# Three modulation pieces moved from the first FFN to the end of the retention stage, and four instructions reordered around the first layer

## The chip, the cores and the metric

One core of a Trainium2 chip (trn2) runs the whole program in one launch. The metric is device time in microseconds (us), lower is better. Engines are written as the profile writes them: PE (TensorE matmul), PEld (its weight load), DVE (VectorE), ACT (ScalarE), POOL (GpSimd), SP (SyncE, which issues the weight DMAs).

## The reference

A two-layer mixer block is followed by a two-layer conditioned block. All of it is float32, 256 tokens, model width 1024. What matters here, cut:

```python
# first block, layer 0
h = rmsnorm(x, mix_norm_even)
cq, ckv, k_rope, rq, rk, rv, rg = split(h @ w_in_even)      # 1024 x 2720
a = mla(cq, ckv, k_rope, positions, ...)                    # 8 heads, softmax attention
r = silu(rg) * rmsnorm(retention_fwd + retention_bwd)       # 8 heads of 64
x = x + concatenate([a, r]) @ w_out_even                    # 1024 x 1024
x = x + conv_ffn(x, ...)                                    # 1024 -> 2 x 2816 -> 1024
# first block, layer 1: gated linear attention, then a conv_ffn
# second block: every layer is modulated by a condition that no token depends on
mod_x = split(silu(c)     @ w_mod[layer] + b_mod[layer], 6) # 1024 x 6144, two layers
mod_c = split(silu(c_ctx) @ w_mod[layer] + b_mod[layer], 6)
```

## The kernel before, in words

**Weights.** Weight matrices come from DRAM in pieces of up to 1 MB (128 x 2048 float32) through a ring of six slots. SP loads piece n as soon as the user of piece n-6 has released it, strictly in the order in which PE uses the pieces. Most products are made in three passes: ACT casts the piece to a rounded copy (`weights_hi`, L1439, `ring_hi`, three buffers), DVE subtracts it from the piece (`weights_lo`, L2066, `ring_r`), and PE multiplies high by high, high by low and low by high (`mm3`, L408). `hi_upto(n)` and `lo_upto(n)` issue those casts on ACT and DVE up to the n-th split piece; where the call stands in an engine's program is where the cast runs, since each engine takes its instructions in order. The normed input is split in the same way: DVE writes `h`, ACT rounds it (`h_hi`), POOL subtracts (L1329, `h_lo`).

**Modulation pieces.** The product with `w_mod` depends on no token. It is cut into 48 pieces of 1 MB, and `fill(n)` spreads them over the first block. On PE a fill is eight small matmuls (printed as 16 in the profile, 128x256, into bank 7 of PSUM), and then `turn_mod` of the piece before it (4 printed, 128x2). On ACT a fill is a wait for those matmuls, a copy `res<-ps` 128x256 that frees bank 7, and the copy `mods<-ps` 128x4 of the piece before it. So the next fill's matmuls can't start before ACT has made the copy. How many pieces go where is in `FILL` and `FFN_FILL`: 16 in attention, one per step, 4 in retention, 9 in the first FFN (1 ahead of it, 8 in its up steps).

**Opening.** PE makes the input projection in column blocks (`tokens`), each in two halves of 512 rows, one split piece per half. DVE casts piece 0, norms the input (L2046), casts piece 1 with `lo_upto(j + 2)`, then computes the rotary angles from the positions (L2025 to L2244, signal `setup_dve`), two small scalings (L2246, L2248), and the casts of pieces 2 and 3. ACT waits for `setup_dve` (L1606) and then makes sine, cosine and some decay terms, and only behind these the copies of block 0 and the cast of piece 4.

**Attention** has 16 steps (`attend_mla`). At each, PE issues the scores of step n+2, a fill, the transposes of step n's probabilities, and the product of step n-1. The scores of step n+2 use the bank of step n, so they wait for ACT's exponential of step n (L1486). ACT's order in a step is: exponential; in odd steps an exponential of a retention decay (L1491), which waits for DVE (L2115); in steps 6, 8, 10 and 12 a copy of transposed retention inputs (L1439, `h<-ps` 128x512); then the fill's two copies.

**Retention** goes over four head pairs p. PE: `ret_scores`, `ret_pv`, `ret_back` (transposes, L837, and one fill for each p). ACT: copy `ret_oT`, square (L1691), square root (L1477), fill. DVE: decay multiply (L2344), reduction (L2355), gate multiply (L2358), scale (L2364, signal `heads_mix`). Then `turn_mix` transposes the mixed features in four groups (L490), ACT and DVE split them (`pairs_hi`, L1439 and L1565; `pairs_lo`, L2192), and `out_project` multiplies with `w_out_even`. `keep_warm(u, n)` issues n bf16 matmuls whose result is not used (L448).

**First FFN** (`ffn0`): 22 up steps, each one 1 MB piece and 48 matmuls, DVE's convolution (L2409 to L2411), then 11 down pieces.

Of the kernel before, what the change touches and what calls it, by code (L numbers as in the profile page):

```python
# [89 lines left out]
def expert_pieces(x):  # L90
# [6 lines left out]
HALVES = [16, 8]  # L97
MOD_PIECES = 48

FILL = {"attention": 16, "ret": 4, "ffn0": 9, "odd": 1, "gla_gates": 2, "gla": 8,  # L100
        "odd_mix": 3, "ffn1": 5}
FFN_FILL = [(2, 4, 7, 9, 12, 14, 17, 20), range(4, 18, 4)]
PARTS = {"even_act": 0, "even_dve": 0, "odd_act": 7, "odd_dve": 5}
assert sum(FILL.values()) == MOD_PIECES
ONE = [(0, q) for q in range(4)]
# [75 lines left out]
def build(nc, A, out):  # L181
    ctx = ExitStack()
    with ctx:
# [5 lines left out]
        def sig(name):  # L189
            if name not in sems:  # L190
                sems[name] = ctx.enter_context(nc.semaphore(name))
            return sems[name]
# [28 lines left out]
        def col(name, i):  # L221
            return cols[:, COLS[name] + i:COLS[name] + i + 1]
# [3 lines left out]
        warm = sb("warm", [P, 1])  # L226
# [19 lines left out]
        mix0 = area(areaB, 4096, TT, D)  # L246
# [82 lines left out]
        first_split = {}  # L329
# [28 lines left out]
        def _(pe):  # L358
# [86 lines left out]
            def keep_warm(u, n):  # L445

                for _ in range(n):
                    pe.matmul(ps[:, u.bank, :], warm_l, warm_r, start=True, stop=True, skip_group_check=True)  # L448
# [30 lines left out]
                            release(m)  # L479
                    release_with(us[-1])  # L480

            def turn_mix(tag, src, fp, n, bank=None, warm=2):

                u = take(tag, "mixT", fp, bank=bank)
                keep_warm(u, warm)
                pe.wait_ge(sig("heads_mix"), n)
                for f in (2 * fp, 2 * fp + 1):
                    for t in range(TT):
                        at = (f % 2) * T + t * P
                        m = pe.transpose(ps[:, u.bank, at:at + P], src[:, t, f * P:(f + 1) * P], ident)  # L490
                full(m, u)
# [276 lines left out]
            for g in range(3):  # L768
                u = take("mla_cT", g)
# [8 lines left out]
            for half in range(2):  # L778
                v = chunk(Piece("mla_w_uq", 0, 0, CQ, half * 384, (half + 1) * 384), 3 * 384, "p (k c) -> p k c", k=3)
                for t in range(TT):  # L780
                    u = take("mla_q", t, half)
# [6 lines left out]
            for half in range(2):  # L788
                for t in range(TT):
                    u = take("mla_kv", t, half)  # L790
# [6 lines left out]
            for i, (name, src) in enumerate((("qT", qh), ("kT", kx))):  # L797
                pe.wait_ge(sig("mla_heads"), i + 1)
                for t in range(TT):
                    for g in range(2):  # L800
                        u = take("mla", name, t, g)
# [52 lines left out]
            ret_pv(3)  # L854
            turn_mix("even", mix0, 2, 4, 2)
            ret_back(3)
            turn_mix("even", mix0, 3, 6, 3, 8)
            out_project("even_out", ("w_out_even", 0), 1, 2 * (MIXED["even"] + TT), "ffn0", True)


# [70 lines left out]
            for d in range(2):  # L931
                for t in range(TT):
                    u = take("gla_la", d, t)
                    full(mm(ps[:, u.bank, :], gaT[0:2 * GR + 1, t * P:(t + 1) * P], wg[0:2 * GR + 1, d, :]), u)
            parts(1, 1, "odd")
            for t in range(TT):
                u = take("gla_kT", t)
# [7 lines left out]
            for d in range(2):  # L945
                pe.wait_ge(sig("gla_la"), d + 1)
                for t in range(TT):
                    u = take("gla_kd", d, t)
# [7 lines left out]
            for n in range(2 * GH):  # L956
# [13 lines left out]
                u = take("gla_A", n)  # L970
# [20 lines left out]
            for l in range(2):  # L991
# [9 lines left out]
                u = take("gates", l)  # L1001
# [4 lines left out]
                for c in range(2):  # L1006
                    v = split_chunk(Piece(*w, 0, D, 768 + c * 256, 768 + (c + 1) * 256), "p (k c) -> p k c", k=8)
                    for m2 in range(2):
                        u = take("conv", l, 2 * c + m2)
# [12 lines left out]
                for t in both:  # L1022
                    if t < 2 or l == 0:
                        u = take("aqT", l, t)
                        for j in range(4):
                            src = ro[:, t, j * P:(j + 1) * P] if t < 2 else p2[:, t, j * P:(j + 1) * P]
# [86 lines left out]
            u = take("rank")  # L1113
# [321 lines left out]
        def _(act):  # L1435
# [43 lines left out]
            def attend_mla():  # L1479
                for n, (t, hd) in enumerate(MLA):  # L1480
                    L.wait("att_m", n + 1)
                    if n >= 3:

                        look(act, "mla", "pT", n - 3)
                    u = look(act, "mla", "s", n)
                    free(L, act.activation(mla_p[:, n % 3, :], ps[:, u.bank, 0:T], ACT.Exp, bias=stat[:, n:n + 1],  # L1486
                                           scale=MQK ** -0.5, accum_out=stat[:, 16 + n:17 + n]), u, "att_p")
                    if n % 2:
                        x = n // 2
                        L.wait("ret_e", x + 1)  # L1490
                        L.tell(act.activation(decay[:, x, :, :], decay[:, x, :, :], ACT.Exp), "ret_d")  # L1491
                    if n - 1 in RET_AT:
                        t, g = divmod(RET_AT.index(n - 1), 2)
                        u = look(act, "ret_T", t, g)
                        free(L, copy(rT[:, 4 * g:4 * g + 4, t * P:(t + 1) * P],
                                     ps[:, u.bank, :].rearrange("p (a b) -> p a b", a=4)), u, "ret_T")
                    fill(1)

            def attend_pairs(l):

# [42 lines left out]
            def hi_upto(n):  # L1543

                while his[0] < n:
                    weights_hi(his[0])
                    his[0] += 1
# [8 lines left out]
            def pairs_hi(tag, fps, gain):  # L1556

                for fp in fps:
                    u = look(act, tag, "mixT", fp)
                    if gain(2 * fp) is None:  # L1560
                        L.tell(copy(h_hi[:, 0, 2 * fp:2 * fp + 2, :],
                                    ps[:, u.bank, :].rearrange("p (a b) -> p a b", a=2)), "mixT_hi")
                        continue
                    for f in (2 * fp, 2 * fp + 1):
                        L.tell(act.activation(h_hi[:, 0, f, :], ps[:, u.bank, (f % 2) * T:(f % 2 + 1) * T], ACT.Copy,  # L1565
                                              scale=gain(f)), "mixT_hi")
# [19 lines left out]
            def fill(n):  # L1586

                for i in range(filled[0], filled[0] + n):
                    u = look(act, "mod", i)
                    free(L, copy(modrow[:, i % 2, :], ps[:, u.bank, 0:256]), u, "mod_row")  # L1590
                    if i:
                        turned_mod(i - 1)
                filled[0] += n
# [93 lines left out]
            for p in range(4):  # L1687
                u = look(act, "ret_b", p)
                if p >= 2:
                    L.wait("heads_sumsq", 1 + p)  # L1690
                L.tell(act.activation(rsq[:, p % 2, :, :], ps[:, u.bank, 0:T].rearrange("p (a b) -> p a b", a=4),  # L1691
                                      ACT.Square), "heads_sq")
                if p == 2:
                    hi_upto(first_split["even_out"] + 1)
                if p < 3:
                    ret_oT(p + 1)
                L.wait("heads_sumsq", 3 + p)
                rstd(stat[:, 4 * p:4 * p + 4], RD)
                act.sem_inc(sig("heads_rstd"), 1)
                if p < FILL["ret"]:  # L1700
                    fill(1)
                if p == 1:
                    pairs_hi("even", (0, 1), lambda f: None)
            pairs_hi("even", (2, 3), lambda f: col("ret_g", f - 4))
            def project_out(tag, mix, tiles, gain, norm, n, after=None):
                j = first_split[tag]
# [313 lines left out]
        def _(dve):  # L2020
# [50 lines left out]
            def lo_upto(n):  # L2071

                while los[0] < n:
                    weights_lo(los[0])
                    los[0] += 1
# [148 lines left out]
            j = first_split["even_in"]  # L2224
            lo_upto(j + 1)
            norm(1, lambda hf, k: col("mix_even", k), split=True)
            lo_upto(j + 2)

            L.wait("pos_loaded", 16)
            S(copy(posf, posi[:, :]))  # L2230
# [106 lines left out]
            for n in range(6):  # L2337
                if n < 4:
                    for hd in range(2):
                        u = look(dve, "ret_s", n, hd)  # L2340
                        L.wait("ret_d", 2 * n + hd + 1)
                        if n >= 2:
                            look(dve, "ret_o", n - 2)
                        free(L, STT(out=sdec[:, n % 2, hd, :], in0=ps[:, u.bank, :], scalar=RD ** -0.5,  # L2344
                                    in1=decay[:, 2 * n + hd, :, :].rearrange("p a b -> p (a b)"), op0=ALU.mult,
                                    op1=ALU.mult), u, "ret_sdec")
                if n == 3:
                    pairs_lo("even", (0, 1), lambda f: None)
                if 1 <= n <= 4:
                    p = n - 1  # L2350
                    if n == 4:
                        lo_upto(first_split["even_out"] + 1)
                    u = look(dve, "ret_b", p)
                    L.wait("heads_sq", 3 + p)
                    S(dve.tensor_reduce(stat[:, 4 * p:4 * p + 4], rsq[:, p % 2, :, :], AX.X, ALU.add))  # L2355
                    dve.sem_inc(sig("heads_sumsq"), 1)
                    a = EVEN["rg"] + P * p
                    free(L, TTN(mix0[:, :, 512 + P * p:640 + P * p], ps[:, u.bank, 0:T].rearrange("p (a b) -> p a b", a=2),  # L2358
                                pe_[:, :, a:a + P], ALU.mult), u)
                if n >= 2:  # L2360
                    p = n - 2
                    inverted("heads_rstd", 4 + p, stat[:, 4 * p:4 * p + 4])
                    v = mix0[:, :, 512 + P * p:640 + P * p].rearrange("p t (h c) -> p t h c", h=2)
                    L.tell(TTN(v, v, bc(stat[:, 4 * p:4 * p + 4].rearrange("p (t h) -> p t h", t=TT), 3, [P, TT, 2, RD]),  # L2364
                               ALU.mult), "heads_mix")
# [552 lines left out]
```

## Time and profile before

| | |
|---|---|
| median of 3 runs | 2642.38 us (2640.11 to 2644.3) |
| the profiled execution | 2644.3 us, span 2642.5 us |
| PE busy | 2476.5 us, 94% |
| DVE / ACT / POOL busy | 1666.2 / 1280.4 / 533.0 us |
| mean granted TensorE clock | 0.963 |

The span is from the first to the last instruction of the profiled execution; 1.8 us of its time lie around it. PE's share of the span is high, so what matters is the idle time on PE and the matmuls that it issues, stage by stage. The opening lies at 0 to 57 us, attention at 113 to 167, retention to 194, the output projection to 220, the norm to 234, the first FFN's up steps to 370.

### The profile page before, as it was taken

The numbers are of one execution on the slowest core, as the hardware profiler recorded it, in microseconds if no ns is written. First come the engines' busy times: TensorE is split into PE (matmuls) and PEld (weight loads), VectorE is DVE, ScalarE is ACT, GpSimd is POOL, SyncE is SP. The second block draws the span as 40 slices with busy tenths as digits, with TensorE's granted clock in tenths as the row PEclk, the third lists the DMA queues.
The fourth block names the chain that finished last, engine by engine and source line by source line (L and its number), as shares of the span: only waits on it lengthen the run. The fifth ranks groups of instructions, "written<-read, shape, count | busy, mean of one in ns | idle before, by whom it ended". The sixth has DMA issues, their size and how long they took to land.

```text
span 2642.5 us, 37437 instructions
## 1 busy us (share of the span) xinstructions
PE 2476.5 (94%) x14360; PEld 2060.7 (78%) x14360; DVE 1666.2 (63%) x1755; ACT 1280.4 (48%) x1541; POOL 533.0 (20%) x406
## 2 busy tenths in 40 slices
PE   7999999999999998779999989889999999999997
PEld 5668998768998865558889968567887887887886
DVE  6555764446775566643222256657888888888886
ACT  6453444544343445432222133545677676677674
POOL 1003541002541000022002630001232232222321
PEclk9999999999999998689999989888999999999998
DMA  5575654554663310012222213015899889899894
GB/s 197 204 253 185 232 205 154 177 193 150 216 209 106 112 64 9 3 62 96 96 96 96 88 49 127 25 66 193 336 337 353 336 342 348 334 348 352 322 363 174
DMA packets 71328, 502.75 MB, mean 190 GB/s; under 512 B 8176, under 2 KB 8688, under 8 KB 11248
## 3 DMA queue, kind: packets, MB, share of 16 engines
q1 hardware_dynamic: 70128, 496.75, 51.3%
q0 software_dynamic: 1024, 3.61, 0.4%
q8 instruction: 116, 1.90, 0.3%
q14 instruction: 60, 0.49, 0.1%
HBM read 499.28 MB, written 1.05 MB: 189 GB/s over the span
## 4 chain that ended last, share of the span: by engine, by line
PE 83%; DVE 9%; ACT 5%; issue 2%; POOL 1%; DMA 1%; DVEq 0%; ACTq 0%; SPq 0%; PEldq 0%
PE ps L408 80%; DVE ring_r L2066 1%; DVE h L2044 1%; POOL h_r L1329 1%; DVE h L2042 1%; DVE areaA L2036 1%; PE ps L1153 1%; PE ps L448 1%; ACT ring_hi L1439 1%; DVE h L2046 1%; ACT h L1517 1%; DVE areaB L2546 0%; ACT extra_r L1577 0%; DVE temp L2129 0%; DVE h L2632 0%
## 5 line engine op out<-in xcount | busy, mean ns | idle before, releaser
L1439 ACT ACTIVATE ring_hi<-ring 128x2048 fp32r<-128x2048 f32 x427 | 807.3, 1893 | 511.4 <-PE ps L408 504.8
L2796 DVE TENSOR_TENSOR ring_r<-ring,ring_hi 128x2048 fp32r<-128x2048 f32 x264 | 625.2, 2373 | 119.0 <-ACT ring_hi L1439 117.1
L408 PE MATMUL ps<-ring_hi,extra_r 128*128 128x512 f32 (+2 forms) x1808 | 611.4, 395 | 31.8 <-DVE ring_r L2066 19.0
L2066 DVE TENSOR_TENSOR ring_r<-ring,ring_hi 128x2048 fp32r<-128x2048 f32 (+3 forms) x163 | 388.2, 2382 | 220.6 <-ACT ring_hi L1439 206.5
L408 PE MATMUL ps<-extra_r,ring_hi 128*128 128x256 f32 (+1 forms) x1432 | 465.8, 325 | 33.6 <-POOL h_r L1329 20.5
L408 PE MATMUL ps<-h_r,ring_hi 128*128 128x256 f32 (+1 forms) x1432 | 459.6, 321 | 0.0
L408 PE MATMUL ps<-extra_r,ring_r 128*128 128x256 f32 (+1 forms) x1432 | 459.3, 321 | 0.0
L408 PEld LDWEIGHTS ps<-ring_hi,extra_r 128*128 128x128 f32 x1808 | 343.6, 190 | 109.3 <-DVE ring_r L2066 22.0
L408 PE MATMUL ps<-ring_r,extra_r 128*128 128x512 f32 (+2 forms) x1104 | 426.4, 386 | 0.0
L408 PEld LDWEIGHTS ps<-extra_r,ring_hi 128*128 128x128 f32 x1432 | 275.4, 192 | 58.5 <-POOL h_r L1329 23.6
L408 PEld LDWEIGHTS ps<-h_r,ring_hi 128*128 128x128 f32 x1432 | 275.7, 193 | 19.1
L408 PEld LDWEIGHTS ps<-extra_r,ring_r 128*128 128x128 f32 x1432 | 275.2, 192 | 19.0
L1385 POOL TENSOR_TENSOR areaA_r<-areaA,cst 128x256 fp32r<-128x256 f32 x88 | 123.0, 1397 | 588.2 <-ACT areaA L1962 588.2
L408 PEld LDWEIGHTS ps<-ring_r,extra_r 128*128 128x128 f32 x1104 | 211.4, 191 | 38.7 <-issue 0.2
L1329 POOL TENSOR_TENSOR h_r<-h,extra_r 128x256 fp32r<-128x256 f32 x80 | 85.4, 1083 | 449.2 <-ACT extra_r L1439 449.2
L408 PE MATMUL ps<-ring_hi,h_r 128*128 128x512 f32 (+2 forms) x400 | 151.2, 378 | 0.0
L408 PE MATMUL ps<-ring_hi,areaA_r 128*128 128x512 f32 x352 | 137.6, 391 | 6.0 <-ACT areaA L1962 6.0
L408 PE MATMUL ps<-ring_hi,areaB_r 128*128 128x512 f32 x352 | 139.8, 397 | 0.0
L408 PE MATMUL ps<-ring_r,areaA_r 128*128 128x512 f32 x352 | 138.0, 392 | 0.0
L408 PE MATMUL ps<-areaA_r,ring_hi 128*128 128x256 f32 x704 | 127.0, 283 | 0.0
L408 PE MATMUL ps<-areaB_r,ring_hi 128*128 128x256 f32 x704 | 124.4, 280 | 0.0
L2704 DVE TENSOR_TENSOR areaA<-ps,areaB 128x512 f32<-128x512 f32 x22 | 15.2, 692 | 166.9 <-PE ps L408 166.9
(350 smaller groups left out, 3339.4 us busy)
## 6 DMA issues: line engine op xcount, KB each, us to landing
ring<-in_experts SPq DMA_DIRECT2D x264, 1024.0 KB, 4.9
ring<-in_stream SPq DMA_DIRECT2D x202, 1024.0 KB, 4.9
ring<-in_stream SPq DMA_DIRECT2D x6, 512.0 KB, 3.6
areaB<-in_consts POOLq DMA_DIRECT2D x3, 512.0 KB, 4.0
ring<-in_stream SPq DMA_DIRECT2D x2, 576.0 KB, 3.7
res<-in_xT SPq DMA_DIRECT2D x1, 1024.0 KB, 5.7
res<-in_ctxT POOLq DMA_DIRECT2D x1, 1024.0 KB, 7.8
out_xT<-h SPq DMA_DIRECT2D x4, 256.0 KB, 2.2
```

The source lines that it names most:

```text
L408: return pe.matmul(o, l, r, start=start, stop=stop, skip_group_check=True)
L448: pe.matmul(ps[:, u.bank, :], warm_l, warm_r, start=True, stop=True, skip_group_check=True)
L1153: m = pe.transpose(ps[:, 3, s * P:(s + 1) * P], mprod[:, n % 2, s * P:(s + 1) * P], ident)
L1329: pool.tensor_tensor(h_lo[:, hf, k, :], h[:, hf, k, :], h_hi[:, hf, k, :].bitcast(F32), ALU.subtract).then_inc(sig("h_lo"), 1)
L1385: pool.tensor_tensor(hi, mturn[:, n % 2, :], ones[:, 0:1].broadcast_to([P, NM]), ALU.mult).then_inc(sig("moe_hi"), 1)
L1439: return act.activation(dst, src, ACT.Copy)
L1517: free(L, act.activation(pair_p[:, 2 * (n % 2) + hd, 0:w.keys * P], ps[:, u.bank, 0:w.keys * P], ACT.Exp, bias=pair_neg[:, i:i + 1], scale ...
L2036: S(dve.reciprocal(rs, rs))
L2042: S(TTN(h[:, hf, k:k + 4, :], res[:, hf, k:k + 4, :], bc(rs[:, hf * T:(hf + 1) * T], 1, [P, 4, T]), ALU.mult))
L2044: ins = TS(h[:, hf, k, :], h[:, hf, k, :], gain(hf, k), shift(hf, k), ALU.mult, ALU.add)
L2066: L.tell(TTN(ring_lo[:, s, 0:n], ring[:, s, 0:n], ring_hi[:, j % HIS, 0:n].bitcast(F32), ALU.subtract), "weights_lo")
L2796: TTN(ring_lo[:, s, :], ring[:, s, :], ring_hi[:, j % HIS, :].bitcast(F32), ALU.subtract).then_inc(sig("weights_lo"), 1)
```

## The change

Three of the first FFN's nine modulation pieces are made at the end of retention, behind `ret_back(3)` on PE and ahead of the last two feature groups on ACT; the eight warm-up matmuls there become two. The FFN's remaining in-step fills stand at every fourth step. On ACT, each attention step's fill comes before the decay exponential and the transposed-input copy. The two casts of the output projection's first piece move back on both engines: on ACT from ahead of `ret_oT(3)` to behind the fill of p = 2, on DVE from ahead of the last reduction to behind it. In the opening, DVE's cast of piece 1 is no longer made right behind the norm but by the later `lo_upto(j + 4)`.

```diff
-FILL = {"attention": 16, "ret": 4, "ffn0": 9, "odd": 1, "gla_gates": 2, "gla": 8,
+FILL = {"attention": 16, "ret": 4, "even_mix": 3, "ffn0": 6, "odd": 1, "gla_gates": 2, "gla": 8,
         "odd_mix": 3, "ffn1": 5}
-FFN_FILL = [(2, 4, 7, 9, 12, 14, 17, 20), range(4, 18, 4)]
+FFN_FILL = [range(4, 22, 4), range(4, 18, 4)]
...
-            def turn_mix(tag, src, fp, n, bank=None, warm=2):
+            def turn_mix(tag, src, fp, n, bank=None):
                 u = take(tag, "mixT", fp, bank=bank)
-                keep_warm(u, warm)
+                keep_warm(u, 2)
...
             turn_mix("even", mix0, 2, 4, 2)
             ret_back(3)
-            turn_mix("even", mix0, 3, 6, 3, 8)
+            fill(FILL["even_mix"])
+            turn_mix("even", mix0, 3, 6, 3)
             out_project("even_out", ("w_out_even", 0), 1, 2 * (MIXED["even"] + TT), "ffn0", True)
...
# ACT, attend_mla
                     free(L, act.activation(mla_p[:, n % 3, :], ps[:, u.bank, 0:T], ACT.Exp, bias=stat[:, n:n + 1],
                                            scale=MQK ** -0.5, accum_out=stat[:, 16 + n:17 + n]), u, "att_p")
+                    fill(1)
                     if n % 2:
...
                         free(L, copy(rT[:, 4 * g:4 * g + 4, t * P:(t + 1) * P],
                                      ps[:, u.bank, :].rearrange("p (a b) -> p a b", a=4)), u, "ret_T")
-                    fill(1)
...
# ACT, retention
-                if p == 2:
-                    hi_upto(first_split["even_out"] + 1)
                 if p < 3:
                     ret_oT(p + 1)
...
                 if p < FILL["ret"]:
                     fill(1)
+                if p == 2:
+                    hi_upto(first_split["even_out"] + 1)
                 if p == 1:
                     pairs_hi("even", (0, 1), lambda f: None)
+            fill(FILL["even_mix"])
             pairs_hi("even", (2, 3), lambda f: col("ret_g", f - 4))
...
# DVE, opening
             norm(1, lambda hf, k: col("mix_even", k), split=True)
-            lo_upto(j + 2)
 
             L.wait("pos_loaded", 16)
...
# DVE, retention
-                    if n == 4:
-                        lo_upto(first_split["even_out"] + 1)
                     u = look(dve, "ret_b", p)
                     L.wait("heads_sq", 3 + p)
                     S(dve.tensor_reduce(stat[:, 4 * p:4 * p + 4], rsq[:, p % 2, :, :], AX.X, ALU.add))
                     dve.sem_inc(sig("heads_sumsq"), 1)
+                    if n == 4:
+                        lo_upto(first_split["even_out"] + 1)
```

## Rows read from the trace of the kernel before

**Rows 1.** The page: the span.
```profile
span 2642.5 us, 37437 instructions
```

**Rows 2.** Timeline of PE in the opening: start us, us, engine, line, operation, idle before.
```profile
27.80 0.50 PE L408 MATMUL ps<-ring_hi,extra_r 128*128 128x512 f32 x1 [1.09 <-DVE ring_r L2066]
...
44.28 0.80 PE L408 MATMUL ps<-ring_hi,extra_r 128*128 128x512 f32 x1 [5.42 <-DVE ring_r L2066]
```

**Rows 3.** Windows: length, busy of PE, PEld, DVE, ACT, POOL; PEclk, DMA share, GB/s.
```profile
44.20:47.50 3.30, 3.22 (x8) 2.55 (x9) 2.65 (x3) 0.49 (x2) 0.00 (x0) 0.50 0.01 2
```

**Rows 4.** Timeline of DVE in the opening.
```profile
25.14 2.60 DVE L2066 TENSOR_TENSOR ring_r<-ring,ring_hi 128x2048 fp32r<-128x2048 f32 x1
27.79 0.58 DVE L2025 CAST temp<-positions 128x2 f32<-128x2 int32 x1
...
31.04 0.17 DVE L2248 TENSOR_SCALAR cols<-cols 128x8 f32<-128x8 f32 x1
...
41.94 4.62 DVE L2066 TENSOR_TENSOR ring_r<-ring,ring_hi 128x2048 fp32r<-128x2048 f32 x2 [0.16 <-DVE areaA L2025]
```

**Rows 5.** Timeline of POOL in the opening, window 26 to 27 us.
```profile
25.59 2.74 POOL L1329 TENSOR_TENSOR h_r<-h,extra_r 128x256 fp32r<-128x256 f32 x1
```

**Rows 6.** Timeline of ACT in the opening.
```profile
30.87 1.28 ACT L1606 ACT_TABLE_LOAD   x1 [3.30 <-DVE temp L2244]
```

**Rows 7.** Timeline of ACT in attention, steps 8 to 10.
```profile
141.42 0.60 ACT L1439 ACTIVATE h<-ps 128x512 f32<-128x512 f32 x1
143.13 0.38 ACT L1439 ACTIVATE res<-ps 128x256 f32<-128x256 f32 x1 [1.11 <-PE ps L408]
...
143.84 0.47 ACT L1486 ACTIVATE h<-ps,stat 128x256 f32<-128x256 f32 x1
...
145.86 0.63 ACT L1491 ACTIVATE extra<-extra 128x512 f32<-128x512 f32 x1 [1.45 <-DVE extra L2115]
...
147.02 0.17 ACT L1439 ACTIVATE mods<-ps 128x4 f32<-128x4 f32 x1
147.23 0.47 ACT L1486 ACTIVATE h<-ps,stat 128x256 f32<-128x256 f32 x1
```

**Rows 8.** Timeline of PE in attention: the fill of step 9.
```profile
145.09 1.07 PE L408 MATMUL ps<-ring,res 128*32 128x256 f32 x16
```

**Rows 9.** Timeline of ACT at the end of retention.
```profile
184.57 1.91 ACT L1439 ACTIVATE ring_hi<-ring 128x2048 fp32r<-128x2048 f32 x1
...
188.66 0.38 ACT L1691 ACTIVATE areaB<-ps 128x256 f32<-128x256 f32 x1
189.91 0.30 ACT L1477 ACTIVATE stat<-stat,cst 128x4 f32<-128x4 f32 x1 [0.88 <-DVEq L2356]
190.33 0.38 ACT L1439 ACTIVATE res<-ps 128x256 f32<-128x256 f32 x1
...
191.04 0.98 ACT L1565 ACTIVATE extra_r<-ps,cols 128x256 fp32r<-128x256 f32 x2
```

**Rows 10.** Timeline of DVE at the end of retention.
```profile
187.02 2.28 DVE L2066 TENSOR_TENSOR ring_r<-ring,ring_hi 128x2048 fp32r<-128x2048 f32 x1
189.34 0.42 DVE L2355 TENSOR_REDUCE stat<-areaB 128x4 f32<-128x256 f32 x1
```

**Rows 11.** Timeline of PE: the output projection's first matmul.
```profile
194.41 0.47 PE L408 MATMUL ps<-extra_r,ring_hi 128*128 128x256 f32 x1
```

**Rows 12.** Timeline of DVE in the first FFN: starts of three convolution steps.
```profile
250.00 0.54 DVE L2409 TENSOR_SCALAR areaB<-ps,cols 128x256 f32<-128x256 f32 x1 [2.46 <-PE ps L408]
...
255.75 0.54 DVE L2409 TENSOR_SCALAR areaB<-ps,cols 128x256 f32<-128x256 f32 x1 [0.82 <-PE ps L408]
...
263.15 0.54 DVE L2409 TENSOR_SCALAR areaB<-ps,cols 128x256 f32<-128x256 f32 x1 [2.46 <-PE ps L408]
```

**Rows 13.** Timeline of PE in layer 1: two fills.
```profile
521.54 1.49 PE L408 MATMUL ps<-ring,res 128*32 128x256 f32 x16 [2.43 <-ACT res L1439]
...
590.73 1.93 PE L408 MATMUL ps<-ring,res 128*32 128x256 f32 x16
```

## The prediction

> **What bounds the kernel now.** I read the page first for the span and the shares of the engines, then the list of PE's waits over 0 to 60, 110 to 170 and 230 to 380 us, then the timeline of each engine in the stages that the diff touches. PE is busy 94% of the span, so an edit matters only where it opens or closes an idle stretch of PE, or adds or removes matmuls. Four places are touched. In the opening PE stands still for 5.42 us until DVE has cast piece 4 [rows 2], and when it goes on its clock is at the lower of the two levels, 1.2 GHz, for the next 3.3 us [rows 3]. In attention every step runs round a ring of PE and ACT: exponential, scores, fill matmuls, the fill's two copies on ACT, the next exponential [rows 7, 8]. At the end of retention a chain on ACT and DVE leads to the first matmul of the output projection [rows 9 to 11]. In the first FFN's up steps PE has no idle time, and each fill makes a step longer.
>
> **The opening: earlier angles, a later cast of piece 1.** The position work on DVE runs from 27.79 to 31.21 us, 3.42 us, behind the cast of piece 1 that began at 25.14 [rows 4]. Without that cast it starts 2.65 us earlier. ACT's chain begins the moment it is told [rows 6], so it and the decay terms on DVE behind it come 2.65 us earlier too. The price: the cast of piece 1 now starts at 25.14 + 3.42 = 28.56. One such cast takes 2.31 us where POOL is quiet (half of 4.62 [rows 4]), so it ends at 30.9, and PE's second half starts at 30.95 instead of 27.80 [rows 2]. From 27.80 PE works without a break until 44.28 - 5.42 = 38.86, 11.06 us; the same work now ends at 42.0. The new gap ahead of it is about 4.2 us (3.15 more than the 1.09 that stands there). The clock fell in the gap of 5.42, so I let it fall here: half of 3.3 us at PEclk 0.50 is 1.65 us lost [rows 3]. PE then reaches piece 4 at 43.65. Piece 4's casts wait for PE to release a `ring_hi` buffer at the end of the slowed second half (30.95 + 5.6 + 1.65 = 38.2; 5.6 is my estimate of 24 of the matmuls of about 0.23 us), then take 1.92 on ACT and 2.31 on DVE: ready at 42.5, just in time. Before, PE reached the same point at 44.28 and then lost its own 1.65: 45.93. Gain 2.3 us. Bounds: nothing, if piece 4 is late all the same; 3.9 (45.93 - 42.0) if the clock holds in the new gap.
> While DVE's cast of piece 1 ran from 25.14 to 27.74, POOL's last subtraction took 2.74 us [rows 4, 5], and DVE's first position instruction, two elements wide, took 0.58 [rows 4]. The Trainium skill (SBUF — State Buffer, "Who interferes with whom") says that a DVE instruction with two SBUF inputs and a GpSimd one that reads SBUF take a shared port for the whole instruction, and the second fully blocks. By it the position work, now beside POOL's last subtraction, might start up to 0.9 us later and the gain be 1.4; by the rows alone it is 2.3, and I keep that.
>
> **Attention: the fill ahead of ACT's other work.** Before, the decay exponential sits in the time in which ACT waits for the fill's matmuls: they run until 145.09 + 1.07 = 146.16 [rows 8], and the exponential until 146.49 [rows 7]. It costs the ring only the 0.33 us by which it is late, because DVE delivers late. With the fill first, ACT's copy can start at 146.23, 0.07 behind the matmuls as in step 8 (0.38 long, the mods copy 0.5 after its start, ready for the next instruction 0.21 later: 147.02 to 147.23 [rows 7]), thus at 146.94. Then the decay exponential comes in the ring with its 0.63 and 0.03 of handover: next exponential at 147.60 instead of 147.23, +0.37. Seven odd steps have a next one: 2.6 us. In steps 6, 8, 10 and 12 the copy of 0.60 runs at 141.42, wholly inside the wait that ends at 143.13 [rows 7]. Moved behind the fill it lies bare between 143.81 and the exponential at 143.84: +0.63, four times, 2.5 us. Sum +5.1. What is queued behind is the exponential, and PE's scores wait for that, so nothing absorbs it. Bounds: 0, if PE and not ACT closed the ring; 5.8 if the first odd step, where the copy isn't late, pays the full 0.66 and each of the others 0.1 more.
>
> **The end of retention: three fills and two moved casts.** The ACT cast of 1.91 at 184.57 lay in a wait for PE's `ret_pv(3)` and was free. Moved behind the fill of p = 2 it stands ahead of the square at 188.66 [rows 9], which moves to 190.60. DVE's reduction follows at once, for its own cast [rows 10] is now behind it: the 1.25 from square to root shrinks to about 1.0, and the copy of the fourth fill moves from 190.33 to 192.03, +1.70. That copy frees bank 7, so the three new fills can only start then. Each goes round PE and ACT: matmuls 1.07, handover 0.07, copy 0.38, handover 0.06 = 1.58; three are 4.74. The split of the third feature group, at 191.04 before, starts at 191.04 + 1.70 + 4.74 = 197.5, and PE's first matmul of the output projection, 3.37 behind it before [rows 9, 11], at 200.9. Cost 6.4 us. DVE's cast and its `heads_mix` (191.04 + 0.42 for the reduction, 2.3 for the cast, 1.7 for the rest: 195.5) are ready before the last fill is. Six fewer warm-up matmuls save nothing, since they stood in the wait. Bounds: 4.1, if the fills go through at 0.8 less each by not waiting for ACT; 6.4 and the clock's price.
>
> **The clock there.** PE's new wait for bank 7 lasts from about 189.9 to 192.5. Layer 1 has such a case: a fill that stood 2.43 us waiting for ACT's copy, and its matmuls then took 1.49 instead of 1.07; in another stretch 1.93 [rows 13]. So the clock probably falls here too, and 0.86 is then lost on each fill that it reaches. I take one and a half: +1.3. Bounds 0 and 3.4 (a second fall in the wait ahead of the projection).
> The Trainium skill (TensorE: Matmul & The Clock Gate, "Wait — 56ns, not 53.3ns?") gives about 62 ns for each small matmul when the sequencer is the bound, whatever the clock; by that 16 of them would take 1.0 us at both levels and this term would be 0. The trace has 1.07 at one and 1.93 at the other [rows 8, 13], and the measurement decides.
>
> **The first FFN: three fills fewer.** A step without a fill takes 255.75 - 250.00 = 5.75 us, one with a fill 263.15 - 255.75 = 7.40 [rows 12]. A fill costs 1.65, three 4.95. DVE, which has 0.82 idle in the short steps [rows 12], can follow three short ones in a row. Gain 4.95. Nothing else there changes: one fill stays ahead of it, and the pieces' DMAs are issued earlier in a stage where the ring is not empty.
>
> **Sum.** -2.3 + 5.1 + 6.4 + 1.3 - 4.95 = +5.55 us. Against the profiled execution (2644.3, span 2642.5 [rows 1]) that is 2649.9; it was 1.9 above the median, and on the median of 2642.4 it is 2647.9 us. A measurement of this kernel can tell about 0.2%, 5.3 us, from no change; I forecast slower, by hardly more than that.
>
> **Rivals.**
> *The clock holds at the end of retention* (no term of 1.3, a small gain elsewhere): +4.2, 2646.6 us. For it: three PE waits of about 1 us in this trace pass without a fall. Against: rows 13.
> *The opening gains nothing:* the cast of piece 4 waits for PE's later release of the buffer, and PE stands there again. +7.9, 2650.3 us. Against: 42.5 is before 43.65, though by only 1.2.
> *The other side, not slower: PE closes the ring in attention.* If ACT's copies have slack there, the reordering costs 0 and the late decay exponential disappears from the ring, with the total at +0.45 or below: 2642.8 us. It decides from the point at which PE's own work in a step exceeds 3.1 us. Against: PE's scores are recorded as waiting for ACT's exponential.
> *The three fills run at PE's pace* at the end of retention: 4.1 instead of 6.4 and no fall of the clock: +1.95, 2644.4 us. Against: the copy that frees the bank.
>
> **How the numbers follow.** Forecast 0.44, clock holds 0.18, opening gains nothing 0.12, PE closes the ring 0.12, fills at PE's pace 0.08, anything faster by more than 0.2% 0.06 (a full gain of 3.9 in the opening together with one of the two last). The range 2643.5 to 2651.0 leaves out the ring and the faster cases, 0.18, and reaches at its top past the opening's rival. Slower takes the forecast, less a little of it since it sits on the limit, and the opening's rival: 0.52. Same takes the three rivals between and that little: 0.42. Faster 0.06.
>
> **What would show it.** In the profile after: PE's wait ahead of piece 4 gone and one of about 4.2 us ahead of the second half of block 0; in attention exponentials 3.76 us apart from odd to even steps (3.39 before) and 3.73 instead of 3.10 behind steps 6, 8, 10, 12; the first `w_out_even` matmul about 9 us later than before, -2.3 + 5.1 + 6.4, or 10 with the clock; fills 1.58 us apart at the end of retention, the first with a wait for ACT; the FFN's up steps 4.95 shorter in all. The prediction is wrong if the exponentials keep their distance, or if PE waits again for piece 4.

## The result, and the profile after

| | before | after |
|---|---|---|
| median of 14 runs each | 2644.16 us (2637.72 to 2651.09) | 2659.43 us (2651.75 to 2671.57) |
| ratio, 95% interval | | 1.0065 [1.0053, 1.0078] |
| span of the profiled execution | 2642.5 us | 2660.0 us |
| mean granted clock there | 0.963 | 0.957 |

Slower by 0.65%, 15.3 us by the medians, where I had forecast 5.5 us. The direction was right and the size was not: 2659.4 lies 8 us above the top of my range. The changed kernel was executed 33 more times in the course of the study; the median of these 33 is 2661.8 us and that of all 47 is 2661.7 us, 17.3 above the 2644.4 of the kernel before in the experiments. Where an experiment is compared with the changed kernel below, the median of the 47 stands beside that of the 14.

The mean granted clock fell with the change, and it goes with the time. Of the 47 executions, the one with the highest mean clock, 0.963, took 2646.8 us, and the one with the lowest, 0.952, took 2671.6 us. So the first thing to read is where PE ran at the lower level. Three windows of the changed kernel's trace (columns as in [rows 3]; the granted clock is the column before the last two):

```profile
29.60:36.40 6.80, 5.05 (x12) 4.00 (x13) 6.22 (x18) 6.65 (x10) 0.00 (x0) 0.50 0.41 145
162.70:179.80 17.10, 16.88 (x97) 11.38 (x92) 4.38 (x10) 5.55 (x14) 0.00 (x0) 0.50 0.58 213
203.70:220.80 17.10, 15.22 (x84) 9.37 (x86) 8.62 (x12) 8.16 (x15) 0.00 (x0) 0.50 0.61 234
```

The first is the opening's, which before had one of the same length from 40.8 us. The other two are new: the end of attention with the start of retention, and the three moved fills with the start of the output projection. Between 50 and 230 us the kernel before has none.

The next table reads the same chain at eight landmarks in both traces. Its last two columns are two of the experiments below, which keep the changed order of work and add warm-up matmuls in attention, or in attention and ahead of the fills. The column "before" has start times in us; the others have the distance to it:

| landmark | before | after | warm-ups in attention | warm-ups in both |
|---|---|---|---|---|
| first exponential of attention | 115.17 | -1.3 | -2.0 | -0.9 |
| last exponential | 162.12 | +7.2 | +4.0 | +5.1 |
| first decay multiply of retention (L2344) | 167.66 | +11.6 | +4.4 | +5.5 |
| fourth square (L1691) | 188.66 | +13.9 | +6.3 | +7.4 |
| split of the third feature group (L1565) | 191.04 | +22.3 | +14.7 | +12.4 |
| first convolution of the FFN (L2409) | 235.36 | +24.7 | +17.0 | +12.4 |
| last convolution of the FFN | 370.87 | +18.3 | +10.6 | +6.0 |
| span | 2642.50 | +17.5 | +11.3 | +3.0 |

Behind the first FFN nothing is changed; there the distance moves by several us with falls of the clock that come at other places in each trace, and so one span is a poor witness where a median is at hand.

**Attention**, the line that answers to [rows 7]. Timeline of ACT in the changed kernel, steps 6 to 8:

```profile
136.69 0.39 ACT L1440 ACTIVATE res<-ps 128x256 f32<-128x256 f32 x1 [1.82 <-PE ps L408]
137.19 0.17 ACT L1440 ACTIVATE mods<-ps 128x4 f32<-128x4 f32 x1
137.40 0.60 ACT L1440 ACTIVATE h<-ps 128x512 f32<-128x512 f32 x1
138.20 0.47 ACT L1487 ACTIVATE h<-ps,stat 128x256 f32<-128x256 f32 x1 [0.21 <-ACT h L1440]
...
140.59 0.39 ACT L1440 ACTIVATE res<-ps 128x256 f32<-128x256 f32 x1 [1.82 <-PE ps L408]
141.09 0.17 ACT L1440 ACTIVATE mods<-ps 128x4 f32<-128x4 f32 x1
141.30 0.63 ACT L1493 ACTIVATE extra<-extra 128x512 f32<-128x512 f32 x1
141.96 0.47 ACT L1487 ACTIVATE h<-ps,stat 128x256 f32<-128x256 f32 x1
```

ACT now stands idle for 1.82 us in front of the fill's copy and does the other work behind it, with the next exponential waiting: 138.20 to 141.96 is 3.76 us, as forecast. The exponential behind the copy starts 0.80 us later than before (134.30 to 138.20 is 3.90, where it was 3.10), not 0.63: 0.60 for the copy and 0.20 of handover. PE pays at its side. Timeline of PE, the last such step and the fills behind it:

```profile
161.78 0.70 PE L408 MATMUL ps<-areaB 96*128 96x256 f32 x2 [0.99 <-ACT h L1487]
162.41 1.67 PE L408 MATMUL ps<-ring,res 128*32 128x256 f32 x16
...
166.24 1.94 PE L408 MATMUL ps<-ring,res 128*32 128x256 f32 x16
```

PE waited 0.99 us for the exponential, the clock fell at 162.7, and the fill's matmuls went from 1.07 [rows 8] to 1.94. It rose again at 179.8. This was the last of four such waits; behind the first three, at 138.82, 146.48 and 154.13, it had stayed up. In a chain in which ACT waits for PE and PE for ACT, each of PE's parts then takes longer in full.

**The end of retention**, which answers to [rows 9, 11]. Timeline of ACT and then of PE:

```profile
200.59 1.91 ACT L1440 ACTIVATE ring_hi<-ring 128x2048 fp32r<-128x2048 f32 x1
202.53 0.38 ACT L1692 ACTIVATE areaB<-ps 128x256 f32<-128x256 f32 x1
203.61 0.30 ACT L1478 ACTIVATE stat<-stat,cst 128x4 f32<-128x4 f32 x1 [0.70 <-DVEq L2355]
204.03 0.38 ACT L1440 ACTIVATE res<-ps 128x256 f32<-128x256 f32 x1
```

```profile
204.55 1.94 PE L408 MATMUL ps<-ring,res 128*32 128x256 f32 x16 [2.54 <-ACT res L1440]
...
207.37 1.93 PE L408 MATMUL ps<-ring,res 128*32 128x256 f32 x16
...
210.17 1.93 PE L408 MATMUL ps<-ring,res 128*32 128x256 f32 x16
```

The wait for bank 7 is there with 2.54 us where I had 2.6, the square and the copy stand where the working put them relative to each other, and the clock fell in the wait. But it reached all three fills and not one and a half: they stand 2.8 us apart. It then stayed down into the projection, whose first matmuls are 0.21 us apart instead of 0.12. The first of them starts at 217.72, 23.3 us later than before, where I had 9 to 10.

**The opening** answers to [rows 2]:

```profile
31.35 0.80 PE L408 MATMUL ps<-ring_hi,extra_r 128*128 128x512 f32 x1 [3.82 <-DVE ring_r L2068]
```

No wait for piece 4 is left. PE goes on at 31.35 (forecast 30.95), since DVE's position work met POOL's last subtraction and took 0.4 us longer, and then ran at the lower level until 36.4.

**The first FFN** answers to [rows 12]: the short steps are as short as before, and three of them stand in a row. Timeline of DVE:

```profile
284.70 0.55 DVE L2410 TENSOR_SCALAR areaB<-ps,cols 128x256 f32<-128x256 f32 x1 [2.46 <-PE ps L408]
290.46 0.54 DVE L2410 TENSOR_SCALAR areaB<-ps,cols 128x256 f32<-128x256 f32 x1 [0.82 <-PE ps L408]
296.22 0.54 DVE L2410 TENSOR_SCALAR areaB<-ps,cols 128x256 f32<-128x256 f32 x1 [0.82 <-PE ps L408]
```

### The profile page after: what moved, and what is told of

Read it like the earlier page. It is cut to its first block, busy times and chain, and to the rows that moved or that the text cites. A ratio compares the mean times of both kernels' runs of the same rounds, so it can differ in the third digit from the quotient of the medians.

```text
span 2660.0 us, 37401 instructions
## 1 busy us (share of the span) xinstructions
PE 2489.6 (94%) x14331; PEld 2070.2 (78%) x14354; DVE 1666.1 (63%) x1755; ACT 1280.6 (48%) x1541; POOL 531.3 (20%) x406
## 4 chain that ended last, share of the span: by engine, by line
PE 84%; DVE 8%; ACT 5%; issue 2%; POOL 1%; DMA 1%; DVEq 0%; ACTq 0%; SPq 0%; PEldq 0%
PE ps L408 81%; DVE h L2046 1%; DVE ring_r L2068 1%; POOL h_r L1330 1%; ACT ring_hi L1440 1%; DVE h L2044 1%; PE ps L448 1%; DVE areaA L2038 1%; PE ps L1154 1%; DVE h L2048 1%; ACT h L1518 1%; DVE areaB L2547 0%; ACT extra_r L1578 0%; DVE temp L2131 0%; DVE h L2633 0%
```

## The experiments

All times are medians of several runs against runs of the kernel before on the same chip, which took 2644.4, 2644.1 and 2644.4 us in the three groups. "Clock theory" is: the waits that the change opens on PE let its clock fall, and that is most of what my sum lacks. "Serial theory", the rival, is: the lacking time is longer chains of work, and the falls are incidental. Each experiment has one trace; a fall that a trace shows or lacks is that of one execution, and the medians say how far the others agree.

### Each part alone

Attention's order on ACT alone:

```diff
                     free(L, act.activation(mla_p[:, n % 3, :], ..., ACT.Exp, ...), u, "att_p")
+                    fill(1)
                     if n % 2:
...
-                    fill(1)
```

> The kernel before, with the fill ahead of the decay exponential and the transposed-input copy on ACT in attention, and nothing else. Clock theory: the longer ACT part makes the ring 5.4 us longer in all, and the wait that it opens on PE in each step lets the granted clock fall near the end of attention, which costs some 7 us more up to the first retention product: +10 to +13 us in runs in which it falls, +10 in the median. Serial theory (the rival): only the longer ring, +5.4 us, and no fall of the clock between 113 and 180 us.

Measured: 2662.45 us in the median of 6 runs (2651.2 to 2666.79), 1.0066 [1.0046, 1.0086], +18.0 us. The profiled execution is one of its shortest, span 2649.7. Its last exponential comes 9.1 us later than before and its first decay multiply 13.5 later; the clock was down from 164.4 to 181.5:

```profile
164.40:181.50 17.10, 17.10 (x98) 11.41 (x92) 4.31 (x10) 5.54 (x14) 0.00 (x0) 0.50 0.60 211
```

So this part alone costs about as much as the whole change. The serial theory's 5.4 is out: the interval starts at 12. The median is above the clock theory's too; with 6 runs over 16 us it doesn't say by how much.

The opening alone:

```diff
             norm(1, lambda hf, k: col("mix_even", k), split=True)
-            lo_upto(j + 2)
```

> The kernel before, without the early cast of piece 1 in the opening, and nothing else. Both theories: the first exponential of attention comes 1.3 us earlier than before (the profile of the changed kernel has 113.88 against 115.17), so -1.3 us; my prediction had -2.3.

Measured: 2640.87 us, 0.9988 [0.9976, 1.0001], -3.6 us by the medians, not clear of no change. In its profile the first exponential is 0.4 us early. PE waited 4.57 us ahead of the second half and none ahead of piece 4. The fourteen traces of this study settle the sign: the first exponential starts at 113.2 to 114.8 us in the seven with this edit and at 115.1 to 116.9 in the seven without, on average 1.5 us earlier.

The end of retention with the FFN alone (the fills, both casts, the warm-ups; the diff ahead of the prediction):

> The kernel before, with the end of retention and the first FFN as in the changed kernel (three fills moved, two casts moved, two warm-up matmuls in place of eight). Serial theory: 6.6 us at the end of retention, less 4.95 in the FFN, +1.7 us, fills 1.58 us apart. Clock theory: the wait of 2.5 us for bank 7 lets the clock fall for all of the train and the start of the projection, fills 2.8 us apart and 2.2 us more in the projection: +6 to +8 us.

Measured: 2651.35 us, 1.0025 [1.0016, 1.0034], +6.9 us. The clock was down over the fills and the start of the projection:

```profile
194.10:211.20 17.10, 16.08 (x88) 10.01 (x89) 8.62 (x12) 7.65 (x14) 0.00 (x0) 0.50 0.57 218
```

The whole change without attention's part:

> The changed kernel with attention's order on ACT as before. Serial theory: +1.7 - 1.3 = +0.4 us against the kernel before. Clock theory: +5 to +7. In both the attention steps are 3.10 and 3.39 us apart again, and the clock stays at its upper level from 50 to 200 us.

Measured: 2649.12 us, 1.0023 [1.0009, 1.0037], +4.7 us. Its exponentials keep the distances of before (3.10 and 3.39 us, each within 0.02). With it, the reordering in attention costs 10.3 us inside the full change (2659.43 - 2649.12), 12.5 by the median of the 47.

### The clock held up by warm-up matmuls

The changed kernel with warm-ups in the attention steps, put where PE has time because it later waits for ACT:

```diff
                     u = take("mla", "pT", n, bank=3)
+                    keep_warm(u, 4 if n - 1 in RET_AT else 2 * (n % 2))
```

> The changed kernel, with two bf16 warm-up matmuls on PE in each odd attention step and four in steps 6, 8, 10 and 12, placed ahead of the transposes, where PE later waits for ACT's exponential; their result is not used. Clock theory: the ring keeps its length (3.76 us from odd to even steps), the fall near the end of attention is gone, the first retention product comes 7 us earlier than in the changed kernel's profile: 2650 to 2653 us in the median against 2659 to 2662 for the changed kernel. Serial theory: the warm-up matmuls save nothing, 2659 us or more.

Measured: 2655.61 us, 1.005 [1.0034, 1.0067], 3.8 us less than the changed kernel by its 14 executions and 6.0 by its 47. Its interval overlaps that of the changed kernel, so the median alone doesn't decide. The traces do: in the table above, the chain is 7.2 us shorter up to the first decay multiply than in the changed kernel, as the clock theory has it, with 32 matmuls more. The fall at the end of retention is still there.

With ten more ahead of the moved fills:

```diff
             ret_back(3)
+            u3 = take("even", "mixT", 3, bank=3)
+            keep_warm(u3, 10)
             fill(FILL["even_mix"])
-            turn_mix("even", mix0, 3, 6, 3)
+            turn_mix("even", mix0, 3, 6, u=u3)
```

> As the one before, and with ten warm-up matmuls between the last retention transposes and the first of the three moved fills, where PE waits 2.5 us for bank 7. Clock theory: no fall at the end of retention either, fills 1.58 us apart instead of 2.8, no slow start of the projection: 5 to 6 us less than the one before, 2645 to 2648 us, which is the sum that my prediction had without a term for the clock. Serial theory: no gain over the one before.

Measured: 2652.17 us, 1.0033 [1.0016, 1.005], +8.1 us against before, 7.3 less than the changed kernel (9.5 by the 47); the two intervals don't meet. Its windows, and ACT's fill copies:

```profile
113.00:167.00 54.00, 50.18 (x457) 30.87 (x456) 24.74 (x62) 23.27 (x70) 0.00 (x0) 1.00 0.76 265
167.00:200.00 33.00, 32.29 (x270) 18.19 (x272) 16.72 (x30) 13.55 (x33) 0.00 (x0) 1.00 0.55 204
200.00:225.00 25.00, 23.21 (x199) 20.98 (x192) 12.01 (x16) 11.93 (x14) 0.00 (x0) 1.00 0.60 213
```

```profile
197.58 0.38 ACT L1443 ACTIVATE res<-ps 128x256 f32<-128x256 f32 x1
...
199.30 0.38 ACT L1443 ACTIVATE res<-ps 128x256 f32<-128x256 f32 x1 [1.05 <-PE ps L408]
...
203.45 1.99 ACT L1569 ACTIVATE extra_r<-ps,cols 128x256 fp32r<-128x256 f32 x4
```

The clock is 1.00 throughout these windows, and the fills are 1.72 us apart instead of 2.8. Matmuls whose result nobody uses take 7 us or more off: the serial theory can't have that. The +8.1 that remains is close to the 7.5 of chain length that this trace shows against before (+12.4 at the first convolution, less the 4.95 of the FFN). My sum for that was +4.25, so the expectation of 2645 to 2648 was too low as well. The trace is of one of its shorter executions (2647.4); they reach up to 2657.2, so in others the clock may fall still, which wasn't traced.

### Which of the waits lets it fall

The copy alone behind the fill (steps 6, 8, 10, 12), and the decay exponential alone behind it (odd steps). In the second the two branches also change places, which changes nothing, since no step takes both:

```diff
# e9: copy behind the fill            # e10: decay exponential behind the fill
                     if n % 2:        |                     if n - 1 in RET_AT:
                         ...          |                         ...
+                    fill(1)          | +                    fill(1)
                     if n - 1 in ...: |                     if n % 2:
                         ...          |                         ...
-                    fill(1)          |
```

> The kernel before, with the fill ahead of the transposed-input copy in attention steps 6, 8, 10 and 12 alone (the decay exponential stays ahead of the fill). The ring is 0.80 us longer in four steps: +3.2 us. Clock theory: a wait of about 1 us opens on PE in these four steps, and if it is these long waits that let the clock fall, the median is +8 or more; if it needs the waits of the odd steps too, +3.2.

Measured: 2650.19 us (2646.33 to 2662.45), 1.0022 [1.0007, 1.0037], +5.8. The profiled execution, 2660.6 us long, is at its slow end, and shows a fall behind each of the four steps. Timeline of PE at the first and windows over all four:

```profile
138.69 0.70 PE L408 MATMUL ps<-areaB 96*128 96x256 f32 x2 [0.99 <-ACT h L1486]
139.31 1.72 PE L408 MATMUL ps<-ring,res 128*32 128x256 f32 x16
```

```profile
139.60:146.40 6.80, 6.80 (x48) 4.22 (x40) 1.47 (x5) 1.43 (x5) 0.00 (x0) 0.50 0.62 222
149.80:156.60 6.80, 6.80 (x48) 4.18 (x40) 2.20 (x6) 1.43 (x5) 0.00 (x0) 0.50 0.60 220
160.10:166.90 6.80, 6.80 (x48) 4.08 (x36) 1.37 (x5) 1.33 (x5) 0.00 (x0) 0.50 0.57 216
170.30:187.40 17.10, 16.88 (x99) 11.42 (x90) 4.45 (x10) 5.13 (x14) 0.00 (x0) 0.50 0.58 207
```

> The kernel before, with the fill ahead of the decay exponential in the odd attention steps alone (the transposed-input copy stays ahead of the fill). The ring is 0.37 us longer in six steps and 0.61 in one: +2.8 us. Clock theory: waits of 0.4 us alone are too short to let the clock fall, so +3; if the sum of many short waits does it, +8 or more.

Measured: 2646.78 us (2644.99 to 2650.53), 1.0011 [1.0002, 1.002], +2.4: the longer ring (2.4 in its profile, from the first exponential to the first decay multiply) and no fall between 50 and 230 us:

```profile
113.00:167.00 54.00, 47.68 (x461) 30.33 (x459) 26.43 (x65) 24.65 (x75) 0.00 (x0) 1.00 0.78 282
```

The two medians are 3.4 us apart and their intervals overlap. One profile is of the longest of its kernel's executions and the other of the shortest, so the traces overstate the contrast. But none of the eleven executions without the moved copy is more than 3.8 us above their median, while those with it reach 12.3 above theirs. So of the two halves of the reordering it is most likely the copy, with its wait of 0.99 us on PE, that brings the clock down, in some executions and not in others; the decay exponential's 0.4 us did not by itself, nor did the two waits of 0.85 us near the start of attention in the same trace.

The reordering alone with the warm-ups:

> The attention reordering alone on the kernel before (which measured +17.5 us in the median of 6 runs, 2651 to 2667), with the warm-up matmuls in the waits that it opens. Clock theory: only the longer ring is left, +6.4 us, and the granted clock stays up from 50 to 200 us. Serial theory: as without them, +17.

Measured: 2653.18 us, 1.0033 [1.002, 1.0045], +8.8, and 9.3 less than without the warm-ups, whose interval starts just above where this one ends. Its profile has no fall between 50 and 230 us, and its chain is 6.4 us longer from the first exponential to the first decay multiply. The 2.4 us between that and the median are not explained; a clock that falls in some of its executions would be one way.

### The casts

The fills moved and the warm-ups reduced, but the casts of the projection's first piece left in their places:

> The kernel before with the three fills moved and the eight warm-up matmuls made two, but both casts of the projection's first piece left where they were. If the moved casts cost what my prediction said, this is 1.7 to 1.9 us faster than the kernel with the casts moved too (2651.35 median), and the wait for bank 7 ahead of the train is 0.7 us instead of 2.5. Clock theory: with a wait that short the clock stays up in the train in most runs, and the whole is +0 to +2 us against the kernel before; serial theory: +0 as well, since the train is 4.74 and the FFN gives back 4.95, but then the kernel with the casts moved should have been +1.7 and it measured +6.6.

Measured: 2644.37 us, 1.0008 [0.9992, 1.0023]: no change. Beside the same with the casts moved (2651.35) the two casts cost 7.0 us, where the working gave them 1.7. Timeline of PE, and a window over the fills and the start of the projection:

```profile
190.96 1.07 PE L408 MATMUL ps<-ring,res 128*32 128x256 f32 x16 [0.78 <-ACT res L1440]
```

```profile
194.10:211.20 17.10, 15.31 (x129) 13.70 (x129) 10.09 (x10) 9.16 (x12) 0.00 (x0) 1.00 0.63 241
```

The wait for bank 7 is 0.78 us instead of 2.54, the clock stays at 1.00, and the three fills cost 5.2 us, which the FFN's 4.95 pays back. This is the trace of the shortest of the twelve executions (2635.8), but the sum of these two, +0.2, is also what their median shows. The casts lengthen the chain by 1.9 and with it the wait: in all four traces with 2.54 us of it and no warm-ups ahead of the fills the clock fell there.

### A version that keeps the gains

The opening's edit, and in attention the decay exponential moved to the next even step, where it fits into ACT's wait for the fill:

```diff
-                    if n % 2:
-                        x = n // 2
-                        L.wait("ret_e", x + 1)
-                        L.tell(act.activation(decay[:, x, :, :], ..., ACT.Exp), "ret_d")
+                    if n >= 2 and n % 2 == 0:
+                        decay_exp(n // 2 - 1)      # the same two lines
...
             attend_mla()
+            decay_exp(7)
```

> The kernel before with the opening as in the changed kernel, and in attention the decay exponential of each odd step moved into the following even step, ahead of that step's fill, where ACT waits for the fill's matmuls. Nothing else is changed. Both theories: the ring closes at 3.10 us in every step, seven times 0.29 less, -2.0 us, and -1.3 to -3 in the opening: 3 to 5 us faster than the kernel before, about 2640 us.

Measured: 2639.95 us, 0.9986 [0.9969, 1.0002], -4.1 us by the medians, its interval just short of clear. Timeline of ACT:

```profile
139.35 0.63 ACT L1482 ACTIVATE extra<-extra 128x512 f32<-128x512 f32 x1
140.01 0.60 ACT L1439 ACTIVATE h<-ps 128x512 f32<-128x512 f32 x1
141.05 0.38 ACT L1439 ACTIVATE res<-ps 128x256 f32<-128x256 f32 x1 [0.44 <-PE ps L408]
```

Both fit, and 0.44 us of the wait is left. From the first exponential to the last it is 45.6 us instead of 47.0, 1.4 less where 2.0 were expected. With one fill more ahead of the FFN and seven instead of eight in its steps:

```diff
-FFN_FILL = [(2, 4, 7, 9, 12, 14, 17, 20), range(4, 18, 4)]
+FFN_FILL = [(2, 5, 8, 11, 14, 17, 20), range(4, 18, 4)]
```

> The kernel with the opening's edit and the decay exponential in the even steps (2640.0 median), and one of the eight in-step fills of the first FFN moved into the norm's wait ahead of it, where PE has ten warm-up matmuls and no work. A fill costs 1.65 us in a step and there ends 0.3 us behind ACT's first rounding: -1.3 us against that kernel, 5 to 6 us faster than the kernel before.

Measured: 2640.15 us, 0.9983 [0.9973, 0.9992], -4.3 us: faster than both kernels, but no faster than the one without the moved fill, so that edit gave nothing. Window behind the moved fill:

```profile
231.70:235.10 3.40, 3.40 (x16) 3.40 (x17) 0.36 (x1) 0.00 (x0) 0.63 (x1) 0.50 0.00 0
```

The FFN's up steps are 1.4 us shorter. But the way from the first decay multiply to the first convolution is 1.6 longer than in the trace without the moved fill, and it ends in this stretch at the lower level, which the other trace doesn't have.

## Why the prediction was wrong

**The opening** was forecast at -2.3. Mechanism right: the wait for piece 4 went, one of 3.8 to 4.6 us came ahead of the second half, the clock fell in it. In the changed kernel's profile the gain at the first exponential is 1.3: PE went on 0.4 later, behind DVE's two 48-element products, which took 1.00 us beside POOL's subtraction instead of 0.53, and then stayed at the lower level for 5.05 us instead of 3.3, which is 0.9 more lost. On average over the traces the gain is 1.5. By medians, alone, it is 3.6 with no change just inside its interval.

**Attention** was forecast at +5.1, and here is the step that failed: this part of the sum has no term for the clock. I wrote that "PE's scores wait for that, so nothing absorbs it", priced ACT's side of the ring by it, and never asked what the wait that it opens on PE does to PE's clock, though I priced just such a wait at the end of retention. The ring itself came to +6.0, a little above my bound of 5.8 (0.80 and not 0.63 in the four copy steps, and 0.6 in the first odd step). The clock, which I had at nothing, added 6.5 in the profiled execution: 2.5 us in the last two steps and 4.0 of the 4.4 up to retention's first multiply. So this stretch of the chain came to +12.9 there.

**The end of retention** was forecast at +6.4 and +1.3 for the clock. Chain: +1.9 for the casts (1.7 forecast) and 5.0 for the fills (4.74; their period is 1.72 us when the clock holds, because the next fill's matmuls wait for PE's own `turn_mod` as well, by the place of that instruction), 6.9. Clock: 3.4 on the fills and 2.4 in the projection, 5.8 instead of 1.3. Undersized for two reasons: I let the lower level reach one and a half fills, and it lasted 17.1 us; and I kept the second part only as a bound. The rows from layer 1 [rows 13] had the right price for a fill but not how long the state holds in this stage.

**The first FFN** gave back 4.95 as forecast; the other 1.4 us in the table are a fall at 235.3 us that the kernel before had in its profiled execution and the changed one had not. Traces with the up steps of before and no such fall take 134.0 us from the first convolution to the last, where the trace before has 135.5; the changed kernel takes 129.1, which is 4.9 less.

**The sum.** Chain length: forecast +4.25, measured +8.1 with the clock held (median), 7.5 from the traces (12.4 - 4.95). Clock: forecast 1.3, measured 7.3 between the medians with and without warm-ups (9.5 by the 47), and 12.3 between the two traces at the first convolution (24.7 - 12.4: 6.5 in attention and behind it, 5.8 at the end of retention). I had a rival in which the clock falls less and none in which it falls more; that is what put 2659 outside the range. Of the rivals, that the clock holds, that PE closes the ring in attention, that the opening gains nothing and that the fills run at PE's pace are refuted by the traces.

**What stays open.** The three parts alone sum to 21 us and the whole is 15 by its 14 executions and 17 by its 47; with medians that move by some us that is no contradiction, but it isn't explained. Why the same wait of 0.99 us is followed by a fall in one place and not in another, and why a fall lasts 6.8 us in some places and 17.1 in others, was not tried.

## What to carry to other kernels

In a ring in which two engines take turns, work put behind the hand-off is paid in full, and work put into the wait ahead of it is free: the same two ACT instructions lengthened the chain by 6 us in one place and shortened it by 1.4 in the other. When an edit lengthens another engine's part, look at what PE does meanwhile. A wait of 1 us in four of the steps was enough here to halve its clock for a while, in the traces and, to go by the times, in many executions; in the trace of the changed kernel that cost about as much as the added work itself (6.5 us beside 6.0). Before moving a fill into an idle stretch, ask when the buffer that it needs comes free: two casts that lengthened the chain by 1.9 us cost 7, because they stood ahead of the copy that frees the bank.

## What the runs showed of the hardware

The granted clock fell behind single PE waits of 0.99 us in attention in all three traces that have them without warm-ups: behind the fourth of four in two, behind each of the four in one. The three waits ahead of those fourth ones passed without a fall, as did waits of 0.4 us in every second step and two of 0.85. In the wait of 2.54 us for bank 7 it fell in all four traces without warm-ups ahead of the fills. In six traces it stayed down for 17.1 us, over stretches in which PE was recorded 89 to 100% busy. The trace with 32 warm-up matmuls in attention's waits has no fall there, and with ten more ahead of the fills none there either. The same 16 small matmuls took 1.07 us at the upper level and 1.94 at the lower. DVE's two 48-element products took 1.00 us beside POOL's subtraction and 0.53 without it.
